# Two attentions in groups of a head pair and query tile, with joint maxima and split sums

## Chip, core and metric

One core of one Trainium2 chip runs the whole program. The metric is the device time of one execution in microseconds (us); the runs of a kernel are given by their median.

## What is computed

The program is two blocks in float32 on 512 tokens of width 1024. The change touches two attentions and what prepares the second one.

```
# first block, layer 2: 16 heads of 64, causal, with a decay
s = q_blk @ k.T * 64**-0.5 + cum_q - cum_k ; mask ; softmax ; @ v
# second block, layer 1: 16 query heads, 4 key/value heads, no mask
q = rope(rmsnorm(q)) ; k = rope(rmsnorm(k))
s = q @ k.T * 64**-0.5 ; softmax ; @ v ; @ w_o
```

The other layers (a state space mixer, four feed-forward parts, a gated MLP with mixing over tokens) stay as they are.

## The kernel before

Every large matrix product is made of three passes of split operands (high times high, high times low, low times high). SyncE loads weight units of 512 KB into a ring of four, ScalarE writes their high part (`whi`, line 544), GpSimd the low part (`wlo`, line 512), TensorE multiplies. Each engine has its program written out by hand, in its own order, and semaphores couple them; an engine never passes a wait.

**Attention** (`pe_attn`, `act_attn`, `dve_attn`, called twice: A = 0 causal with N = 128 to 512 columns by query tile, A = 1 with 512 always). A step n is one head and one query tile of 128 rows; n runs over 64 steps, the two heads of a pair taking turns. TensorE makes the scores of step n in one of three PSUM banks, VectorE takes the row maximum (`rowst`, line 1394), ScalarE the exponential with its row sum (line 797, into one of six `pbuf` buffers). Three steps later TensorE transposes the result block by block (line 1916), ScalarE copies the even steps to SBUF (line 805) and VectorE the odd ones (line 1401), and TensorE multiplies with v ("weighs", line 1889, 16 small matmuls per query tile of a pair) into one of two output banks. Once per pair VectorE writes the reciprocals of the eight sums, each repeated 64 times, in one operation of 512 columns (`rdup`, line 1409); TensorE transposes them (the "spread", line 1901), VectorE copies them (line 1383) and multiplies the pair's output with them (line 1386).

**Projection of the second attention** (`pe_t_x`, `act_qkv`, `dve_qkv`). TensorE makes three parts of four units: heads 0 to 7 (PSUM banks 0 to 3), heads 8 to 15 (banks 4 to 7), then keys and values (banks 0 to 3 again, once `q_step` has reached 16, which is VectorE's first read of the last token tile of part one). ScalarE squares a part when its four units are done; VectorE sums, inverts, and applies norm and rope in five operations for each of four token tiles, into `q_tok` and `k_tok`.

**Builds** turn rope results into `qS`, `kS` and `kL`, which hold q (high and low part, one above the other over the 128 partitions) and k high and k low. In the kernel before TensorE transposes q_tok or k_tok (line 1941), ScalarE writes the high part (lines 852, 854), VectorE subtracts it for the low part (lines 1496, 1499). Three builds come ahead of the attention, nine between its steps (`QK_AT`).

Of the kernel before, what the change touches and what calls it, by code (L numbers as in the profile page):

```python
# [46 lines left out]
SBANKS = 3  # L47
TBANK, OBANK, RBANK = 3, 5, 7
PSLOTS = 6
TSLOTS = 8  # L50
LEAD = 3
# [28 lines left out]
QK = [("q", 0, 4), ("q", 1, 5), ("k", 0, 6)]  # L80
QK_AT = {}
for _p in range(6):
    QK_AT[8 * _p + 1] = len(QK)
    QK.append(("q", _p + 2, 7))
    if _p % 2 == 0:
        QK_AT[8 * _p + 7] = len(QK)
        QK.append(("k", _p // 2 + 1, 7))
QK_OF = {(_kind, _x): _j for _j, (_kind, _x, _) in enumerate(QK)}
QK_DONE = [sum(2 if _kind == "q" else 1 for _kind, _, _ in QK[:_j + 1]) for _j in range(len(QK))]

# [29 lines left out]
def build_in(ctx, nc, a, out):  # L120
# [122 lines left out]
    v2 = arena("v2", [P, NT, 256], 64)  # L243
    q_tok = arena("q_tok", [P, NT, D], 48)
    oT2 = arena("oT2", [P, KD, T], 32)
    k_tok = arena("k_tok", [P, NT, 4, 2, HD], 68)
    cs = arena("cs", [P, NT, 2, HD], 76)
    qkg = arena("qkg", [P, 2, HD], 78)
    gcs = arena("gcs", [P, 2, NT, 2, HD], 79)
# [20 lines left out]
    def sem(name):  # L270
# [40 lines left out]
    at_rc = sem("at_recip_copied")  # L311

    q_sq, q_sum, q_std, q_step, v_ev, qk_tp, qk_hi, qk_lo, qkg_in, q_tab = (
        sem(n) for n in ("q_sq", "q_sum", "q_std", "q_step", "v_ev", "qk_tp", "qk_hi", "qk_lo", "qkg_in", "q_tab"))
# [472 lines left out]
    def act_attn(act, A, ptb, causal, hook=None, build=None):  # L787
        B, G = 64 * A, 32 * A
        for n in range(64 + LEAD):
            if n == 56 and hook:  # L790
                hook()
            if n < 64:
                N = (n % 8 // 2 + 1) * P if causal else T
                act.wait_ge(at_max, B + n + 1)
                if n >= PSLOTS:
                    act.wait_ge(at_tp, B + n - PSLOTS + 1)
                act.activation(pbuf[:, n % PSLOTS, 0:N], ps[:, n % SBANKS, 0:N], ACT.Exp, bias=rowst[:, 0, n:n + 1],
                               accum_out=rowst[:, 1, n:n + 1]).then_inc(at_exp, 1)
            m = n - LEAD
            if m >= 0 and m % 2 == 0:  # L800
                N = (m % 8 // 2 + 1) * P if causal else T
                act.wait_ge(at_tp, B + m + 1)
                if m >= TSLOTS:
                    act.wait_ge(at_pv, G + (m - TSLOTS) // 2 + 1)
                act.activation(ptb[:, m % TSLOTS, 0:N], ps[:, TBANK, 0:N], ACT.Copy).then_inc(at_pt_a, 1)
            if build:
                build(n - 1)
# [13 lines left out]
    def act_qkv(act):  # L821
# [4 lines left out]
        for e in range(13):  # L826
            if e < 12:
                act_whi(act, S + AHEAD, e, e % 4)
            if e and e % 4 == 0:
# [16 lines left out]
    def act_qk_hi(act, j):  # L846
        kind, x, bank = QK[j]
        act.wait_ge(qk_tp, j + 1)
        if kind == "q":
            for b in range(2):  # L850
                r = slice(64 * b, 64 * b + 64)
                act.activation(qS[r, (2 * x + b) % 8], ps[r, bank], ACT.Copy, scale=HD ** -0.5).then_inc(qk_hi, 1)
        else:
            act.activation(kS[:, x], ps[:, bank], ACT.Copy).then_inc(qk_hi, 1)
# [104 lines left out]
    def _(act):  # L959
# [41 lines left out]
        for t in range(NT):  # L1001
            act.wait_ge(res_done, 12 + t + 1)
            for h in range(2):
                if 2 * t + h:
# [9 lines left out]
                 build=lambda n: act_qk_hi(act, QK_AT[n]) if n in QK_AT else None)  # L1014
# [363 lines left out]
    def dve_attn(dve, A, oT, ptb, causal, hook=None, build=None):  # L1378
        B, G = 64 * A, 32 * A

        def pv_out(pr):
            dve.wait_ge(at_r, 8 * A + pr + 1)
            dve.tensor_copy(rinv_t[:], ps[:, RBANK]).then_inc(at_rc, 1)
            dve.wait_ge(at_pv, G + 4 * pr + 4)
            dve.wait_ge(at_rc, 8 * A + pr + 1)
            dve.tensor_tensor(oT[:, pr], ps[:, OBANK + pr % 2], rinv_t[:], ALU.mult).then_inc(at_o, 1)

        for n in range(64 + LEAD):
            if n == 58 and hook:
                hook()  # L1390
            if n < 64:
                N = (n % 8 // 2 + 1) * P if causal else T
                dve.wait_ge(at_s, B + n + 1)
                dve.tensor_reduce(rowst[:, 0, n:n + 1], ps[:, n % SBANKS, 0:N], AX.X, ALU.max, negate=True).then_inc(at_max, 1)  # L1394
            m = n - LEAD
            if m >= 0 and m % 2:
                N = (m % 8 // 2 + 1) * P if causal else T
                dve.wait_ge(at_tp, B + m + 1)
                if m >= TSLOTS:
                    dve.wait_ge(at_pv, G + (m - TSLOTS) // 2 + 1)  # L1400
                dve.tensor_copy(ptb[:, m % TSLOTS, 0:N], ps[:, TBANK + 1, 0:N]).then_inc(at_pt_d, 1)
            if build:
                build(n - 1)
            if n >= 9 and n % 8 == 1:
                pr = n // 8 - 1
# [5 lines left out]
            if n >= 14 and n % 8 == 6:  # L1411
                pv_out(n // 8 - 1)
        pv_out(7)
# [25 lines left out]
    def dve_qkv(dve):  # L1439
# [12 lines left out]
        for hh in range(3):  # L1452
# [10 lines left out]
            for t in range(NT):  # L1463
# [4 lines left out]
                twice = lambda x: x[:, 0:w].rearrange("p (h d) -> p h d", d=HD).unsqueeze(2).to_broadcast([P, nh, 2, HD])  # L1468
# [13 lines left out]
                if hh == 2:  # L1482
                    step(dve.tensor_tensor(k_tok[:, t], twice(ra), twice(rb), ALU.add))
                else:
                    step(dve.tensor_tensor(q_tok[:, t, hh * HALF:(hh + 1) * HALF], ra[:, 0:w], rb[:, 0:w], ALU.add))
        assert n == 60
        for j in range(3):
            dve_qk_lo(dve, j)

    def dve_qk_lo(dve, j):  # L1490
        kind, x, bank = QK[j]
        dve.wait_ge(qk_hi, QK_DONE[j])
        if kind == "q":
            for b in range(2):
                r, other = slice(64 * b, 64 * b + 64), slice(64 - 64 * b, 128 - 64 * b)
                dve.scalar_tensor_tensor(qS[other, (2 * x + b) % 8], ps[r, bank], HD ** -0.5, qS[r, (2 * x + b) % 8].bitcast(F32),
                                         ALU.mult, ALU.subtract).then_inc(qk_lo, 1)
        else:
            dve.tensor_tensor(kL[:, x], ps[:, bank], kS[:, x].bitcast(F32), ALU.subtract).then_inc(qk_lo, 1)
# [74 lines left out]
    def _(dve):  # L1574
# [56 lines left out]
        dve_attn(dve, 1, oT2, ptb2, False, hook=lambda: dve_first_splits(dve, "o", oT2),  # L1631
# [449 lines left out]
```

## Time and profile before

| | us |
|---|---|
| median of 3 runs | 3074.87 (3074.86 to 3079.23) |
| profiled execution | 3078.62 |
| its span, first to last instruction | 3076.5 |
| TensorE busy in the span | 2840.0 (92%) |
| VectorE, ScalarE, GpSimd busy | 1421.2, 1083.6, 1142.1 |
| mean granted TensorE clock | 0.966 |

The span is what the trace shows; the profiled execution's time has 2.1 us around it. A busy share tells little on its own here: the three engines behind TensorE matter where TensorE waits for them. Lines with L and a number are lines of the kernel above.

### The profile page before, as it was taken

To read this page: it belongs to the slowest core of one execution; us is meant where nothing else is said; L and a number is where in the kernel's file an instruction comes from. 1 tells how busy PE (TensorE), PEld (TensorE's weight loads), DVE (VectorE), ACT (ScalarE), POOL (GpSimd) and SP (SyncE) were. 2 spreads that over 40 slices of the span, in tenths; PEclk is the share of its full clock that TensorE was granted. 3 is DMA by queue.
4 is the path that set the end of the run, shared out by engine and by line. 5 is a ranking of instruction groups with operands and counts; after the bars stand their busy time and mean duration, and the time that the engine had idled before them with its cause. 6 is when DMAs were issued, how large, how long until landed. Compare 5 with 4: busy or idle time off the path is not lost.

```text
span 3076.5 us, 37311 instructions
## 1 busy us (share of the span) xinstructions
PE 2840.0 (92%) x13390; PEld 2312.3 (75%) x13390; DVE 1421.2 (46%) x1617; ACT 1083.6 (35%) x1529; POOL 1142.1 (37%) x466
## 2 busy tenths in 40 slices
PE   7998799999989988999967888999989988989999
PEld 6786577778867667778856667888878876878887
DVE  4323738775273657776357765123220145331232
ACT  4322233333333443334333544223344222432332
POOL 3442043344434113335423013445444434434443
PEclk9998799999989999999989999999999999999999
DMA  5331035763323004674212003323323331323232
GB/s 146 89 96 55 14 95 179 218 186 101 96 77 89 28 25 140 216 223 128 89 59 69 1 15 88 97 89 98 94 82 102 109 97 48 96 79 98 89 96 75
DMA packets 314313, 297.67 MB, mean 97 GB/s; under 512 B 11932, under 2 KB 246632, under 8 KB 314088
## 3 DMA queue, kind: packets, MB, share of 16 engines
q1 hardware_dynamic: 299784, 235.64, 26.0%
q10 hardware_dynamic: 14432, 60.70, 5.9%
q8 instruction: 65, 1.06, 0.1%
q14 instruction: 32, 0.26, 0.0%
HBM read 294.21 MB, written 2.10 MB: 96 GB/s over the span
## 4 chain that ended last, share of the span: by engine, by line
PE 46%; issue 35%; POOL 13%; DVE 5%; ACT 1%; POOLq 0%; DMA 0%; ACTq 0%; DVEq 0%
POOL wlo L512 13%; PE ps L1735 8%; PE ps L1736 8%; PE ps L1737 8%; PE ps L1652 6%; PE ps L1650 6%; PE ps L1651 6%; DVE nrm L1424 1%; DVE gk L1549 1%; PE ps L1889 0%; PE ps L1916 0%; PE ps L1761 0%; DVE rowst L1394 0%; PE ps L1763 0%; PE ps L1762 0%
## 5 line engine op out<-in xcount | busy, mean ns | idle before, releaser
L512 POOL TENSOR_TENSOR wlo<-raw,whi 128x1024 fp32r<-128x1024 f32 x444 | 1118.6, 2526 | 1875.9 <-ACT whi L544 1875.7
L1650 PE MATMUL ps<-xhi,whi 128*128 128x512 f32 x1824 | 714.0, 391 | 22.3 <-POOL wlo L512 20.8
L1651 PE MATMUL ps<-xlo,whi 128*128 128x512 f32 x1824 | 710.3, 389 | 0.0
L1652 PE MATMUL ps<-xhi,wlo 128*128 128x512 f32 x1824 | 709.9, 389 | 0.0
L544 ACT ACTIVATE whi<-raw 128x1024 fp32r<-128x1024 f32 x444 | 465.3, 1050 | 277.2 <-PE ps L1737 198.5
L1735 PE MATMUL ps<-whi,ahi 128*128 128x512 f32 x1184 | 465.5, 393 | 18.4 <-issue 11.2
L1736 PE MATMUL ps<-wlo,ahi 128*128 128x512 f32 x1184 | 463.6, 392 | 0.0
L1737 PE MATMUL ps<-whi,alo 128*128 128x512 f32 x1184 | 463.4, 391 | 0.0
L1650 PEld LDWEIGHTS ps<-xhi,whi 128*128 128x128 f32 x1824 | 342.6, 188 | 104.3 <-POOL wlo L512 32.1
L1652 PEld LDWEIGHTS ps<-xhi,wlo 128*128 128x128 f32 x1824 | 342.6, 188 | 71.5
L1651 PEld LDWEIGHTS ps<-xlo,whi 128*128 128x128 f32 x1824 | 342.6, 188 | 70.0
L1735 PEld LDWEIGHTS ps<-whi,ahi 128*128 128x128 f32 x1184 | 224.2, 189 | 67.9 <-issue 20.2
L1737 PEld LDWEIGHTS ps<-whi,alo 128*128 128x128 f32 x1184 | 224.0, 189 | 47.1
L1736 PEld LDWEIGHTS ps<-wlo,ahi 128*128 128x128 f32 x1184 | 224.2, 189 | 46.0
L1232 DVE TENSOR_TENSOR alo<-hid_mlp,ahi 128x1024 fp32r<-128x1024 f32 x60 | 78.7, 1312 | 233.3 <-ACT ahi L695 233.3
L1514 DVE SCALAR_TENSOR_TENSOR hid_mlp<-ps,relu 128x512 f32 (+1 forms) x64 | 44.3, 692 | 292.1 <-ACT relu L869 292.1
L1735 PE MATMUL ps<-whi,xhi 128*128 128x512 f32 x416 | 164.3, 395 | 7.6 <-DVE xlo L1045 4.6
L1736 PE MATMUL ps<-wlo,xhi 128*128 128x512 f32 x416 | 163.6, 393 | 0.0
L1737 PE MATMUL ps<-whi,xlo 128*128 128x512 f32 x416 | 163.5, 393 | 0.0
L695 ACT ACTIVATE ahi<-hid_mlp 128x1024 fp32r (+1 forms) x60 | 63.7, 1061 | 196.2 <-PE ps L1737 196.2
L768 ACT ACTIVATE gs<-gt 128x512 f32<-128x512 f32 x44 | 27.8, 632 | 291.8 <-DVE gt L1319 291.8
L869 ACT ACTIVATE relu<-ps 128x512 f32<-128x512 f32 x64 | 38.3, 599 | 240.1 <-PE ps L1652 240.1
(263 smaller groups left out, 3189.8 us busy)
## 6 DMA issues: line engine op xcount, KB each, us to landing
adaraw<-in_ada_w ACTq DMA_DIRECT2D x64, 768.0 KB, 5.8
raw<-in_ffn_w_up SPq DMA_DIRECT2D x88, 512.0 KB, 3.8
raw<-in_mlp_w_in SPq DMA_DIRECT2D x64, 512.0 KB, 4.0
raw<-in_mlp_w_out SPq DMA_DIRECT2D x64, 512.0 KB, 3.7
raw<-in_gmlp_w_in SPq DMA_DIRECT2D x48, 512.0 KB, 3.8
raw<-in_sc_ssm_w_in SPq DMA_DIRECT2D x44, 512.0 KB, 3.8
raw<-in_ffn_w_down SPq DMA_DIRECT2D x44, 512.0 KB, 3.7
raw<-in_fox_w_in SPq DMA_DIRECT2D x24, 512.0 KB, 3.7
```

What stands on the lines that cost most here:

```text
L512: pool.tensor_tensor(wlo[:, j], raw[:, j], whi[:, j].bitcast(F32), ALU.subtract).then_inc(w_lo, 1)
L544: act.activation(whi[:, s], raw[:, s], ACT.Copy).then_inc(w_hi, 1)
L695: act.activation(ahi[:, (m0 + j) % 2], x, ACT.Copy).then_inc(a_hi, 1)
L869: act.activation(relu[:, j % 2], ps[:, bank_f(j)], ACT.Relu).then_inc(relu_done, 1)
L1232: dve.tensor_tensor(alo[:, s], x, ahi[:, s].bitcast(F32), ALU.subtract).then_inc(a_lo, 1)
L1514: dve.scalar_tensor_tensor(hid_mlp[:, bass.ds(e, 1)], ps[:, bank_f(j):bank_f(j) + 1], 0.0, relu[:, j % 2:j % 2 + 1], ALU.max, ALU.mult).th ...
L1650: pe.matmul(out, lh, rh, start=start, stop=False)
L1651: pe.matmul(out, lh, rl, start=False, stop=False)
L1652: return pe.matmul(out, ll, rh, start=False, stop=stop)
L1735: pe.matmul(out, lh[:, k, c], wh[:, k], start=st, stop=False, skip_group_check=True)
L1736: pe.matmul(out, lh[:, k, c], wl[:, k], start=False, stop=False, skip_group_check=True)
L1737: ins = pe.matmul(out, ll[:, k, c], wh[:, k], start=False, stop=False, skip_group_check=True)
```

## The change

A group g is now one query tile of one head pair; there are 32. TensorE makes both scores (four score banks, two per group), VectorE takes the maxima of both heads in one operation over two banks, ScalarE makes both exponentials on that one signal. The transposes come two groups behind (LAG = 2), weighing one more group behind. There is one output bank instead of two. The sums are inverted as eight columns and then copied to 512.

The q and k parts are split before they are transposed: VectorE writes the roped tile to `roped` (two buffers), ScalarE copies its high part to `qsp` or `ksp`, VectorE subtracts the low part, and a build is then four transposes and one copy. `act_rope_hi(hh)` stands in ScalarE's block of the part after hh. Twelve builds come ahead of the attention (all four key heads, high and low, and q heads 0 to 3), twelve (one q head each) between its groups.

```diff
-SBANKS = 3
-TBANK, OBANK, RBANK = 3, 5, 7
+TBANK, OBANK, RBANK = 4, 6, 7
-LEAD = 3
+LAG = 2
-QK = [("q", 0, 4), ("q", 1, 5), ("k", 0, 6)]
+BUILDS = ([("q", _h, 4 + _h) for _h in range(4)]
+          + [(("kh", "kl")[_j % 2], _j // 2, 4 + _j % 4) for _j in range(8)])
+        BUILD_AT[4 * _p + 1 + 2 * _b] = len(BUILDS)
+        BUILDS.append(("q", 2 * _p + 4 + _b, RBANK))
...
 act_attn
+        for g in range(32 + LAG):
+            if g == 28 and hook:
+                hook()
+            if g < 32:
+                act.wait_ge(at_max, G + g + 1)
+                for n in (2 * g, 2 * g + 1):
+                    if n >= PSLOTS:
+                        act.wait_ge(at_tp, B + n - PSLOTS + 1)
+                    act.activation(pbuf[:, n % PSLOTS, 0:N], ps[:, n % 4, 0:N], ACT.Exp, bias=rowst[:, 0, n:n + 1],
+                                   accum_out=rowst[:, 1, n:n + 1]).then_inc(at_exp, 1)
+            w = g - LAG
+            if w >= 0:
+                act.wait_ge(at_tp, B + 2 * w + 1)
+                if w >= 4:
+                    act.wait_ge(at_pv, G + w - 3)
+                act.activation(ptb[:, 2 * w % TSLOTS, 0:N], ps[:, TBANK, 0:N], ACT.Copy).then_inc(at_pt_a, 1)
             if build:
-                build(n - 1)
+                build(g)
...
 act_qkv
+                if hh:
+                    act_rope_hi(act, hh - 1)
                 act.wait_ge(q_sum, 5 * hh + 4)
...
-        for j in range(3):
-            act_qk_hi(act, j)
+        for j in range(4):
+            act_build(act, j)
+        act_rope_hi(act, 2)
+        for j in range(4, FIRST_BUILDS):
+            act_build(act, j)
...
 dve_attn
+            if g < 32:
+                dve.wait_ge(at_s, G + g + 1)
+                dve.tensor_reduce(rowst[:, 0, 2 * g:2 * g + 2], ps[:, 2 * (g % 2):2 * (g % 2) + 2, 0:N], AX.X, ALU.max,
+                                  negate=True).then_inc(at_max, 1)
...
+            if g % 4 == 1 and g > 4:
+                pr = g // 4 - 1
                 dve.wait_ge(at_exp, B + 8 * pr + 8)
+                dve.reciprocal(rowst[:, 2, 8 * pr:8 * pr + 8], rowst[:, 1, 8 * pr:8 * pr + 8]).then_inc(at_rv, 1)
                 if pr:
                     dve.wait_ge(at_r, 8 * A + pr)
-                dve.reciprocal(rdup[:].rearrange("p i (b d) -> p (i b) d", d=HD),
-                               rowst[:, 1, 8 * pr:8 * pr + 8].unsqueeze(2).to_broadcast([P, 8, HD])).then_inc(at_rinv, 1)
+                dve.wait_ge(at_rv, 8 * A + pr + 1)
+                dve.tensor_copy(rdup[:].rearrange("p i (b d) -> p (i b) d", d=HD),
+                                rowst[:, 2, 8 * pr:8 * pr + 8].unsqueeze(2).to_broadcast([P, 8, HD])).then_inc(at_rinv, 1)
+            if g % 4 == 2 and g > 4:
+                pv_out(g // 4 - 1)
...
 dve_qkv
+                step(dve.tensor_tensor(x, ra[:, 0:w], rb[:, 0:w], ALU.add))
+                if t:
+                    dve_rope_lo(dve, hh, t - 1)
+            dve_rope_lo(dve, hh, NT - 1)
...
+    def dve_rope_lo(dve, hh, t):
+        dve.wait_ge(q_hi, 4 * hh + t + 1)
...
 pe_attn
+        for g in range(32 + LAG + 1):
+            if g < 32:
+                if g >= 2:
+                    pe.wait_ge(at_exp, B + 2 * g - 2)
+                for b in range(2):
+                    ins = scores(pe, 2 * (g // 4) + b, g % 4, 2 * (g % 2) + b)
+                ins.then_inc(at_s, 1)
+            w = g - LAG
+            if 0 <= w < 32:
+                pe.wait_ge(at_exp, B + 2 * w + 2)
+                for b in range(2):
+                    if w:
+                        pe.wait_ge(at_pt_d if b else at_pt_a, G + w)
+                    for c in range(w % 4 + 1 if causal else NT):
+                        ins = pe.transpose(ps[:, TBANK + b, c * P:(c + 1) * P],
+                                           pbuf[:, (2 * w + b) % PSLOTS, c * P:(c + 1) * P], ident)
+                    ins.then_inc(at_tp, 1)
+            if w >= 1:
+                weigh(w - 1)
+                if w % 4 == 0:
+                    spread(w // 4 - 1)
             if build:
-                build(n)
+                build(g)
```

## Rows read from the trace of the kernel before

**Rows 1.** The page, chain that ended last: shares of the span by engine.
```profile
PE 46%; issue 35%; POOL 13%; DVE 5%; ACT 1%; POOLq 0%; DMA 0%; ACTq 0%; DVEq 0%
```
**Rows 2.** Busy time by stretch: PE, PEld, DVE, ACT, POOL, then granted clock, DMA, GB/s.
```profile
1678.00:1686.00 8.00, 5.51 (x17) 4.17 (x18) 5.38 (x8) 3.44 (x6) 0.00 (x0) 0.51 0.00 0
1681.50:1822.00 140.50, 114.04 (x963) 88.39 (x964) 107.52 (x135) 74.01 (x178) 2.35 (x1) 0.95 0.00 1
```
**Rows 3.** Timeline, first attention: start, duration, engine, line, operation [idle before].
```profile
1093.63 3.34 DVE L1409 RECIPROCAL rdup<-rowst 128x512 f32<-128x512 f32 x1
...
1105.75 3.34 DVE L1409 RECIPROCAL rdup<-rowst 128x512 f32<-128x512 f32 x1
...
1112.78 1.02 PE L1927 MATMUL ps<-kh,qh 128*128 128x512 f32 x2
...
1113.70 0.39 PE L1916 MATMUL ps<-consts,pbuf 128*128 128x128 f32 x2
```
**Rows 4.** Who waited for whom, 1022 to 1122: total us, times, longest.
```profile
PEld ps L1916 <- ACT pbuf L797: 10.1, 15, 1.6
```
**Rows 5.** Groups by line and shape, VectorE, whole span: busy us, mean ns | idle before.
```profile
L1409 DVE RECIPROCAL rdup<-rowst 128x512 f32<-128x512 f32 x16 | 53.5, 3345 | 0.7 <-ACT pbuf L797 0.6
...
L1165 DVE TENSOR_TENSOR mbuf<-ps,sm 128x1024 f32<-128x1024 f32 x8 | 9.8, 1220 | 1.6 <-PE ps L1835 1.6
...
L1272 DVE RECIPROCAL rstd<-std 128x4 f32<-128x4 f32 x4 | 0.7, 178 | 2.3 <-ACT std L742 2.3
```
**Rows 6.** Timeline, second attention: a stretch without a reciprocal, and its end.
```profile
1709.57 0.59 ACT L805 ACTIVATE ptb<-ps 128x512 f32<-128x512 f32 x1
...
1710.05 0.69 ACT L797 ACTIVATE pbuf<-ps,rowst 128x512 f32<-128x512 f32 x1
1710.30 0.63 PE L1916 MATMUL ps<-consts,pbuf 128*128 128x128 f32 x4 [0.93 <-ACT ptb L805]
...
1711.00 0.39 PE L1935 MATMUL ps<-kL,qS 128*128 128x512 f32 x1
...
1711.37 0.61 ACT L805 ACTIVATE ptb<-ps 128x512 f32<-128x512 f32 x1
1711.43 0.69 DVE L1394 TENSOR_REDUCE rowst<-ps 128x1 f32<-128x512 f32 x1 [0.78 <-PE ps L1935]
1711.76 1.09 PE L1889 MATMUL ps<-ptb,v 128*64 128x128 f32 x16
...
1712.15 0.69 ACT L797 ACTIVATE pbuf<-ps,rowst 128x512 f32<-128x512 f32 x1 [0.17 <-DVE rowst L1394]
...
1712.78 0.50 PE L1934 MATMUL ps<-kS,qS 128*128 128x512 f32 x1
...
1713.12 0.40 PE L1935 MATMUL ps<-kL,qS 128*128 128x512 f32 x1
...
1814.35 1.03 PE L1916 MATMUL ps<-consts,pbuf 128*128 128x128 f32 x8
...
1815.32 1.09 PE L1889 MATMUL ps<-ptb,v 128*64 128x128 f32 x16
```
**Rows 7.** Timeline, projection and rope of the second attention.
```profile
1633.48 0.68 DVE L1475 TENSOR_TENSOR qn<-ps,hsum 128x512 f32<-128x512 f32 x1
...
1635.59 0.69 DVE L1485 TENSOR_TENSOR q_tok<-ra,rb 128x512 f32<-128x512 f32 x1
1636.20 0.68 DVE L1475 TENSOR_TENSOR qn<-ps,hsum 128x512 f32<-128x512 f32 x1
...
1645.28 0.39 PE L1735 MATMUL ps<-whi,xhi 128*128 128x512 f32 x1
...
1646.51 2.04 ACT L836 ACTIVATE sqb<-ps 128x512 f32<-128x512 f32 x4
...
1667.25 1.21 ACT L836 ACTIVATE sqb<-ps 128x256 f32<-128x256 f32 x4 [4.33 <-PE ps L1737]
...
1669.37 0.37 ACT L841 ACTIVATE hsum<-hsum,eps_ln 128x16 f32<-128x16 f32 x1
```

More of the change, by code:

```diff
@@ L788, in act_attn @@
         B, G = 64 * A, 32 * A
-        for n in range(64 + LEAD):
-            if n == 56 and hook:
+        for g in range(32 + LAG):
+            if g == 28 and hook:
                 hook()
[L792 to L805, printed above, removed]
+            if g < 32:
+                N = (g % 4 + 1) * P if causal else T
+                act.wait_ge(at_max, G + g + 1)
[6 more added lines that the diff above has]
+            if w >= 0:
+                N = (w % 4 + 1) * P if causal else T
+                act.wait_ge(at_tp, B + 2 * w + 1)
+                if w >= 4:
+                    act.wait_ge(at_pv, G + w - 3)
+                act.activation(ptb[:, 2 * w % TSLOTS, 0:N], ps[:, TBANK, 0:N], ACT.Copy).then_inc(at_pt_a, 1)
             if build:
-                build(n - 1)
+                build(g)
     def act_square(act, s, h, tiles_ready):
@@ L1376, in dve_fv, with dve_attn @@
                 dve.tensor_copy(vtok[:, t, h * HALF:(h + 1) * HALF], ps[:, 4 * h + t]).then_inc(fv_ev, 1)
-    def dve_attn(dve, A, oT, ptb, causal, hook=None, build=None):
+    def dve_attn(dve, A, oT, ptb, causal, hook=None):
         B, G = 64 * A, 32 * A
@@ L1385, in pv_out @@
             dve.wait_ge(at_rc, 8 * A + pr + 1)
-            dve.tensor_tensor(oT[:, pr], ps[:, OBANK + pr % 2], rinv_t[:], ALU.mult).then_inc(at_o, 1)
-        for n in range(64 + LEAD):
-            if n == 58 and hook:
+            dve.tensor_tensor(oT[:, pr], ps[:, OBANK], rinv_t[:], ALU.mult).then_inc(at_o, 1)
+        for g in range(32 + LAG):
+            if g == 29 and hook:
                 hook()
[L1391 to L1405, printed above, removed]
+            if g < 32:
+                N = (g % 4 + 1) * P if causal else T
+                dve.wait_ge(at_s, G + g + 1)
+                dve.tensor_reduce(rowst[:, 0, 2 * g:2 * g + 2], ps[:, 2 * (g % 2):2 * (g % 2) + 2, 0:N], AX.X, ALU.max,
+                                  negate=True).then_inc(at_max, 1)
+            w = g - LAG
+            if w >= 0:
+                N = (w % 4 + 1) * P if causal else T
+                dve.wait_ge(at_tp, B + 2 * w + 2)
+                if w >= 4:
+                    dve.wait_ge(at_pv, G + w - 3)
+                dve.tensor_copy(ptb[:, (2 * w + 1) % TSLOTS, 0:N], ps[:, TBANK + 1, 0:N]).then_inc(at_pt_d, 1)
+            if g % 4 == 1 and g > 4:
+                pr = g // 4 - 1
@@ L1481, in dve_qkv @@
                 dve.wait_ge(q_step, n)
[L1482 to L1485, printed above, removed]
+                step(dve.tensor_tensor(x, ra[:, 0:w], rb[:, 0:w], ALU.add))
+                if t:
+                    dve_rope_lo(dve, hh, t - 1)
+            dve_rope_lo(dve, hh, NT - 1)
         assert n == 60
[L1487 to L1497, printed above, removed]
-        else:
-            dve.tensor_tensor(kL[:, x], ps[:, bank], kS[:, x].bitcast(F32), ALU.subtract).then_inc(qk_lo, 1)
+        for j in range(4, FIRST_BUILDS):
+            kind, x, bank = BUILDS[j]
+            if kind == "kl":
+                dve.wait_ge(bd_tp, j + 1)
+                dve.tensor_copy(kL[:, x], ps[:, bank]).then_inc(bd_ev_d, 1)
+    def dve_rope_lo(dve, hh, t):
+        dve.wait_ge(q_hi, 4 * hh + t + 1)
+        x = roped[:, t % 2]
+        if hh < 2:
+            dve.tensor_tensor(qsp[:, t, 8 * hh:8 * hh + 8, 1], x.rearrange("p (h d) -> p h d", d=HD),
+                              qsp[:, t, 8 * hh:8 * hh + 8, 0].bitcast(F32), ALU.subtract).then_inc(q_lo, 1)
+        else:
+            dve.tensor_tensor(ksp[:, t, :, 1], x[:, 0:4 * HD].rearrange("p (h d) -> p h d", d=HD).unsqueeze(2)
+                              .to_broadcast([P, 4, 2, HD]), ksp[:, t, :, 0].bitcast(F32), ALU.subtract).then_inc(q_lo, 1)
     def dve_gate(dve, s):
@@ L1883, in weigh @@
             pe.wait_ge(at_pt_d, G + g + 1)
-            if i == 0 and pr >= 2:
-                pe.wait_ge(at_o, 8 * A + pr - 1)
+            if i == 0 and pr:
+                pe.wait_ge(at_o, 8 * A + pr)
             last = i if causal else NT - 1
@@ L1954, in pe_mod, with pe_build_at @@
+    def pe_build_at(pe, g):
+        if g in BUILD_AT:
+            j, pr = BUILD_AT[g], g // 4
+            pe.wait_ge(bd_ev_a, BUILT_ACT[j - 1])
+            if g % 4 == 1 and pr >= 2:
+                pe.wait_ge(at_o, 8 + pr - 1)
+            if g % 4 == 3 and pr >= 1:
+                pe.wait_ge(at_o, 8 + pr)
+            pe_build(pe, j)
     def pe_mod(pe, L):
```

145 lines of the change are left out of this document (67 added, 78 removed).

## The prediction

> **What bounds the kernel now.** I read the page first, for the chain that ended last, then the busy time by stretch, then the timelines of the three stretches that the change touches. The chain is TensorE's own work or its issue time for 81% of the span [rows 1]: whatever makes TensorE wait costs time, and the other engines cost nothing until they do. The change touches three stretches, all on one path because TensorE works through them in order: the first (causal) attention, 1022.5 to 1127.6; the projection with its rope, up to the first score of the second attention at 1681.5; and the second attention, 1681.5 to 1822.0, where TensorE is busy 114 of 140.5 us [rows 2]. The first attention repeats every 12.12 us per head pair [rows 3], and in 1022:1122 (8.2 such periods) its weight loads wait 10.1 us for exponentials [rows 4]; one of its 15 waits, 1.6 us, is in the tail, so about 1.1 us per pair is waiting and 11.0 us is TensorE's own work. The second attention takes 140.5 us for eight pairs, some 16.5 us each between reciprocals.
>
> **Prices.** The reciprocal of 512 columns takes 3.34 us, 16 times. It becomes one of 8 columns (0.18 us for 4 columns) and a copy of 512 columns, at most 0.7 us. VectorE saves about 2.5 us per pair [rows 5]. The Trainium skill ("VectorE: DVE Perf Modes", Rules for kernel authors) says to minimize the count of operations and not to split; by that rule alone one instruction more would cost some tenths. The row says that here the width of the divide is what costs. The joint maximum reads two PSUM banks, which no maximum does now; the bounds are 1.22 us, the two-bank operation of 1024 columns, and 1.38, twice the 0.69 of one maximum [rows 5, 6]. I take 1.22, since it has one fixed part and not two: the maximum saves little, but the exponentials of both heads now start only when it is done.
>
> **Second attention, period.** I write s for the start of a group's scores on TensorE. The first score's two matmuls take 0.34 and 0.23, the second's 0.22 each (full pace, 512 columns at 2.4 GHz); its last matmul ends 0.39 after it starts and VectorE starts 0.04 later [rows 6]. So the maximum starts at s + 1.22, the exponentials at s + 2.47 (1.22 + 0.03 handoff). Two exponentials take 1.34. Only behind them stands the copy of the transposed pair two groups earlier: 0.59, and 0.14 more until the next group's transposes may start [rows 6]. That is s + 4.54. Eight transposes with their gap take 0.97 (1814.35 to 1815.32), weighing 1.02 (1711.76 to 1712.78), then come the scores of the group after next: s + 6.53, so 3.27 us per group, against 3.01 of TensorE's own work (1.02 + 0.97 + 1.02). Even groups carry two builds per pair (0.35 each, four transposes): 13.8 per pair. Odd ones carry the spread (0.39) and a late maximum: VectorE copies and multiplies the old pair's output for 1.40 behind the spread, until s + 5.15, while the next maximum is due at s + 4.67. That gives 13.1 + 0.4 + 0.5 = 14.0 per pair, now 16.5. Walking it from the first score: warm start to group 13 at 42.1, four more pairs to group 29 at 98.0, then both splits of the hook (2.0 us on ScalarE, 2.3 on VectorE, partly covered), tail and last spread: 115.6 us instead of 140.5. **Gain 24.9.** What goes away is the wait behind the reciprocal, and the VectorE subtraction of the q and k builds between scores.
>
> **First attention.** The same round, with sizes by query tile. The long case is the group of tile 3: one score is 0.92 (1112.78 to 1113.70), the maximum starts at s + 2.04, then 1.25, two exponentials 1.34, copy of a 256-column tile 0.37 + 0.14: s + 5.14. TensorE would be there at s + 3.5 (scores 1.84, four transposes 0.54, four weighings 0.37, the next group's scores 0.75), estimates scaled from the same rows [rows 3, 6]. It waits 1.6 us once per pair; the other three groups come in time. Period 11.0 + 1.6 = 12.7, now 12.12: +0.6, over eight pairs +4.9. In the tail the last copy no longer stands behind a 3.34 us reciprocal, and the pipeline is one group longer: -2.5. **Loss 2.4.** One bank for the output instead of two costs nothing here: the first weighing of a pair comes at s + 2.4, the multiply ends at s + 1.8; in the second attention the margin is only 0.1 us.
>
> **Projection and rope.** Here work is added: twelve subtractions of 512 columns on VectorE (0.69 each, 0.61 back to back, as 1635.59 to 1636.20) [rows 7], twelve copies on ScalarE, 12 leading builds instead of 3. Their order matters more. In the half for heads 0 to 7, VectorE's first low part follows tile 1, but ScalarE issues the high part only in its block for the next half, behind TensorE's unit 8 and four squares. So VectorE stops at 1636.2, where tile 2 starts now, and goes on at 1649.15 (squares from 1646.51 for 2.04, copy 0.63) [rows 7]. Tile 3 is read from PSUM at 1649.15 + 0.61 + 2.72 + 0.61 = 1653.1 (2.72 is 1633.48 to 1636.20), done 1653.8. TensorE's third part waits for exactly this and starts at 1653.85 instead of 1645.28: 8.6 us idle. Its work is 21.9 us, ending now at 1667.2 [rows 7]. Idle time also costs clock: TensorE stands still from 1668 to 1678, and the granted clock is then 0.51 until 1686, the 1.2 GHz level [rows 2]. I take 5.3 us at half rate, 2.6 us lost. End: 1678.4. The Trainium skill ("TensorE: Matmul & The Clock Gate", HAM oscillation) says that such waits re-throttle TensorE; without it the sum would be 2.6 lower.
>
> The same happens once more. VectorE has finished tiles 0 and 1 of the second half by 1670 and stops until squares, v copies (2.12, 1667.25 to 1669.37) and the high part are issued: 1678.45 + 2.12 + 0.63 = 1681.2. Two tiles and four low parts: 1689.25. The key part's reduce, root and reciprocal take 2.1 (estimated from today's 2.4, without the wait for the v copies): 1691.4; four tiles at some 1.7 and the low parts: 1700.7. Only then come the eight key builds. Each is 0.7 at the low clock (0.4 at the high one, half of the 0.97 of eight transposes), and the last needs 1.1 for its transposes to land and 0.69 for VectorE's copy: first score at 1707.3 (1705.0 at the high clock) instead of 1681.5. **Loss 25.8.** The builds' evictions on ScalarE (0.5 to 0.6 per two builds) stay behind TensorE. SyncE's loads are unmoved: the four units of the third part are ready, and the next weights are wanted only after the attention.
>
> **Sum.** -24.9 + 25.8 + 2.4 = +3.3 on a span of 3076.5, 3079.8. The profiled execution took 3078.62, of which 2.1 lies around the span; the median of the three runs shown is 3074.87. Added to that median: 3078.2. About 0.2%, 6.15 us, is what a measurement of this kernel can tell from no change (the three runs differ by 4.4).
>
> **Rivals.**
> A, faster: the attentions run at TensorE's own pace, because the copy is not what the transposes wait for. Then the first attention takes 11.0 per pair and loses its tail (-11 instead of +2.4) and the second 13.1 (another -7): 3058. For it: VectorE's load falls by 2.5 per pair. Against: the round of 4.54 + 1.99 is summed from durations in the trace, and it is longer than twice 3.01.
> B, slower: the round through both exponentials is longer than summed, because the two-bank maximum or a handoff costs more. It is gone through 16 times in the second and 8 times in the first attention where it binds; 0.12 us more per round already passes +6.15, and 0.3 us more gives 3085.4. For it: I have no row of a two-bank maximum, the margin at the output bank is 0.1, and sums of this kind leave out small waits.
> C, faster: VectorE's stop in the rope doesn't reach TensorE (the third part's banks are free earlier than I read) and only the added low parts (12 x 0.61 = 7.3), and builds (8 more, 5) count, 12.3 instead of 25.8: 3064.7. Against it: the wait for step 16 stays in the kernel, and both engines work strictly in order.
> D: the reciprocal of 8 columns costs as much as that of 512. Then the second attention gains almost nothing: over 3090. The 4-column row speaks against it [rows 5].
>
> **Chances.** Forecast 0.52 (its own range 3072 to 3084: the clock term 2.6 in the projection, 2.3 in the builds, 0.1 us per round), of which 0.44 lies within 0.2% and 0.08 above. B 0.28, D 0.02, A 0.11, C 0.07. That makes slower 0.38, same 0.44, faster 0.18. The range reaches from C's value to a B of 0.4 us per round, 3064 to 3088; below it lies A, above it D and the worst of B, together under 0.2.
>
> **What would show it.** In the changed profile: TensorE idle some 8 us in the projection, ended by a VectorE multiply of the rope, and a second half low clock after it; VectorE idle from about 1636 to 1649, ended by ScalarE; the first score of the second attention 24 to 28 us later counted from the start of the projection; then 14.0 us per pair, with TensorE's transposes waiting for ScalarE's copy. In the first attention 12.7 per pair and one wait of 1.6 us for that copy. I am wrong if the pairs take 13.1 and 11.0 (A), if no idle stretch stands in the projection (C), or if the reciprocals are still long (D).

## The result and the profile after

The changed kernel takes 3088.63 us (median of 11 runs, 3084.89 to 3092.23), the kernel before 3079.09 us (median of 11, 3074.86 to 3083.41). The ratio is 1.003, 95% interval 1.0022 to 1.0037: slower by 9.5 us or 0.3%. The profiled execution took 3091.49 us with a span of 3089.7, 13.2 us more than the span before. I cut both spans at the same five events: first score of the first attention, first matmul of the output projection behind it, first score of the second attention, first matmul of the projection behind that, end.

| us | before | after | difference | forecast |
|---|---|---|---|---|
| ahead of the first attention | 1022.5 | 1025.6 | +3.1 | 0 |
| first attention | 105.1 | 114.3 | +9.2 | +2.4 |
| up to the second attention | 553.9 | 578.1 | +24.2 | +25.8 |
| second attention | 140.5 | 116.7 | -23.8 | -24.9 |
| behind it | 1254.5 | 1255.0 | +0.5 | 0 |

The ratio's interval leaves out 1, so the change is slower by a little. The first and last lines have the same code in both kernels. In twelve other executions (below) the first is 1017.6 to 1025.8 and the last 1254.5 to 1257.1, so neither says anything of the change.

**Projection and rope.** Timeline of VectorE and TensorE, where [rows 7] show the same events without a stop:

```profile
1646.13 0.69 DVE L1502 TENSOR_TENSOR roped<-ra,rb 128x512 f32<-128x512 f32 x1
1659.63 0.69 DVE L1517 TENSOR_TENSOR qsp<-roped,qsp 128x512 fp32r<-128x512 f32 x1 [12.81 <-ACT qsp L860]
...
1691.23 0.69 DVE L1517 TENSOR_TENSOR qsp<-roped,qsp 128x512 fp32r<-128x512 f32 x1 [13.31 <-ACT qsp L860]
...
1664.30 0.79 PE L1756 MATMUL ps<-whi,xhi 128*128 128x512 f32 x1 [8.32 <-DVE qn L1495]
...
1695.90 3.56 PE L1975 MATMUL ps<-consts,qsp 128*128 128x128 f32 x16 [7.57 <-DVE qn L1495]
1710.68 6.43 PE L1975 MATMUL ps<-consts,ksp 128*128 128x128 f32 x32 [11.22 <-DVE ksp L1520]
1717.99 0.47 PE L1957 MATMUL ps<-kS,qS 128*128 128x512 f32 x1 [0.88 <-DVE kL L1511]
```

VectorE has two roped tiles by 1646.8 and stands for 12.81 us for ScalarE's high copy (L860), and for 13.31 us once more in the second half. TensorE ends the second part at 1655.8 and stands 8.32 us for VectorE's first read of the fourth tile. Then it starts at half pace: a matmul begins every 0.43 us instead of every 0.23, until 1668.3. It stands again before the first four builds (7.57) and the eight key builds (11.22). The granted clock by stretch (columns as in [rows 2]):

```profile
1656.00:1664.00 8.00, 0.00 (x0) 0.00 (x0) 4.30 (x8) 4.67 (x8) 2.34 (x1) 0.64 0.35 121
1664.00:1672.00 8.00, 7.70 (x25) 6.20 (x26) 7.38 (x14) 0.95 (x2) 0.00 (x0) 0.72 0.01 2
1672.00:1688.00 16.00, 16.00 (x73) 13.18 (x71) 5.82 (x9) 3.18 (x3) 7.52 (x3) 1.00 0.22 69
```

**Second attention.** One group's round, from its first score at 1760.40 to the next transposes:

```profile
1760.40 0.50 PE L1957 MATMUL ps<-kS,qS 128*128 128x512 f32 x1
...
1761.64 1.23 DVE L1413 TENSOR_REDUCE rowst<-ps 128x2 f32<-128x1024 f32 x1 [1.47 <-PE ps L1958]
...
1762.90 0.69 ACT L800 ACTIVATE pbuf<-ps,rowst 128x512 f32<-128x512 f32 x1 [1.62 <-DVE rowst L1413]
...
1764.24 0.60 ACT L808 ACTIVATE ptb<-ps 128x512 f32<-128x512 f32 x1
...
1764.98 1.07 PE L1937 MATMUL ps<-consts,pbuf 128*128 128x128 f32 x8
```

The transposes come at s + 4.58 (forecast 4.54), s being the start of the group's first score as in the prediction. The joint maximum takes 1.23 (forecast 1.22). A pair takes 14.04 us from one reciprocal to the next (forecast 14.0). The reciprocal and its copy, in the same groups of VectorE's work as [rows 5]:

```profile
L1429 DVE COPY rdup<-rowst 128x512 f32<-128x512 f32 x8 | 3.4, 428 | 0.8
L1425 DVE RECIPROCAL rowst<-rowst 128x8 f32<-128x8 f32 x8 | 1.5, 192 | 0.0
```

What TensorE waited for here (total us, times, longest), the three largest before and the largest after:

```profile
PE ps L1916 <- ACT ptb L805: 9.3, 8, 3.7
PE ps L1916 <- DVE ptb L1401: 9.2, 7, 3.1
PE ps L1901 <- DVE qS L1496: 5.5, 5, 1.1
...
PE ps L1937 <- ACT ptb L808: 7.8, 12, 1.9
```

The clock changed too. Before, the granted clock was 0.95 in this stretch, with TensorE busy 114.0 us [rows 2]; after, it is full, with nearly the same number of instructions:

```profile
1718.00:1835.00 117.00, 107.78 (x977) 85.10 (x978) 74.79 (x96) 71.28 (x176) 1.36 (x1) 1.00 0.01 1
```

**First attention.** The widest group, and the wait behind it:

```profile
1109.78 1.02 PE L1949 MATMUL ps<-kh,qh 128*128 128x512 f32 x2
...
1111.88 1.23 DVE L1413 TENSOR_REDUCE rowst<-ps 128x2 f32<-128x1024 f32 x1 [0.40 <-PE ps L1950]
...
1114.48 0.38 ACT L808 ACTIVATE ptb<-ps 128x256 f32<-128x256 f32 x1
...
1115.00 1.01 PE L1937 MATMUL ps<-consts,pbuf 128*128 128x128 f32 x6 [1.54 <-ACT ptb L808]
```

That is s + 5.22 (forecast 5.14) and a wait of 1.54 (forecast 1.6). The widest maximum comes every 12.89 us where nothing disturbs it, and twice only after 14.5. The extra 1.6 us is pace: the transposes behind the wait above take 1.01 us for six, 0.85 in the other pairs. TensorE alone by stretch (time, busy, count, granted clock):

```profile
1064.00:1077.00 13.00, 11.46 (x91) 1.00 0.01 2
1077.00:1090.00 13.00, 11.46 (x86) 0.93 0.01 1
1090.00:1103.00 13.00, 11.46 (x82) 0.94 0.00 1
...
1116.00:1129.00 13.00, 11.12 (x77) 0.89 0.00 0
1129.00:1140.00 11.00, 6.48 (x55) 0.82 0.01 1
```

Who waited for whom in all of the first attention, TensorE's matmuls, before and after ([rows 4] show the weight loads, a different queue, so they don't compare with this):

```profile
PE ps L1916 <- ACT ptb L805: 5.3, 7, 1.4
...
PE ps L1937 <- ACT ptb L808: 13.0, 9, 2.4
```

### The profile page after: what moved, and what is told of

Read it like the earlier page. It is cut to its first block, busy times and chain, and to the rows that moved or that the text cites. A ratio compares the mean times of both kernels' runs of the same rounds, so it can differ in the third digit from the quotient of the medians.

```text
span 3089.7 us, 37251 instructions
## 1 busy us (share of the span) xinstructions
PE 2849.7 (92%) x13438; PEld 2323.1 (75%) x13438; DVE 1364.7 (44%) x1565; ACT 1087.8 (35%) x1541; POOL 1141.5 (37%) x466
## 4 chain that ended last, share of the span: by engine, by line
PE 46%; issue 34%; POOL 12%; DVE 5%; ACT 1%; POOLq 0%; DMA 0%; ACTq 0%; DVEq 0%
POOL wlo L514 12%; PE ps L1756 8%; PE ps L1758 8%; PE ps L1757 8%; PE ps L1673 6%; PE ps L1672 6%; PE ps L1671 6%; PE ps L1910 1%; PE ps L1937 1%; DVE nrm L1444 1%; DVE gk L1571 1%; DVE rowst L1413 0%; PE ps L1782 0%; PE ps L1784 0%; PE ps L1783 0%
## 5 line engine op out<-in xcount | busy, mean ns | idle before, releaser
L1671 PE MATMUL ps<-xhi,whi 128*128 128x512 f32 x1824 | 714.6, 392 | 22.2 <-POOL wlo L514 20.7
```

The source lines that it names most:

```text
L1671: pe.matmul(out, lh, rh, start=start, stop=False)
```

## The experiments

The medians are of 5, 11, 5, 5, 11, 4, 8, 4, 4, 11, 11 and 4 runs, in the order of the experiments. Each ratio is to the kernel before as it ran in the same session (medians 3078.95, 3080.73 and 3079.99 for experiments 1 to 4, 5 to 8 and 9 to 12); differences in us are between medians as printed, so 1 or 2 us between sessions are in them. Stretches are from one profiled execution of each kernel, in the order of the table above: first attention, up to the second, second attention.

**1. Copy ahead of the exponentials.**

```diff
 act_attn, for each g
+            [wait for the transposes; copy ptb of group g - 2]
             [wait for the maxima; two exponentials of group g]
-            [wait for the transposes; copy ptb of group g - 2]
```

> The changed kernel with one edit: ScalarE copies the transposed pair of two groups back before, not behind, the two exponentials of a group. Theory (the round through the joint maximum, both exponentials and only then the copy holds TensorE's transposes; 13.0 us of such waits in the first attention, 7.8 in the second, and the 3.2 us of low clock behind them): most of it goes, 18 us (14 to 22) off the changed kernel, about 3070; the first attention repeats every 11.4 us instead of 12.9, the second every 13.1 to 13.3 instead of 14.0, and no low clock is left inside the first. Rival (TensorE is held by something else of the round, the exponentials that free the score banks or VectorE's late maximum, and the copy only happens to end last): the waits change their name, and the time stays within 3 us, 3086 to 3092.

Measured: 3063.44 us (3061.03 to 3064.31), ratio to before 0.9947 (0.9933 to 0.996): 25.2 us off the changed kernel. Stretches 96.4, 578.8, 106.0. The widest maximum comes every 11.19 us, 0.5 us of waits for the copy are left in the first attention, and behind the start TensorE is busy without a gap and at full clock, as here:

```profile
1064.00:1077.00 13.00, 13.00 (x98) 1.00 0.00 0
```

The rival fell: the waits went, they did not change their name. The size is above my bound (14 to 22): not most, but nearly all of the waits and of the low clock inside the pairs went (13.0 + 3.2 + 7.8 = 24.0).

**2. Four roped tiles.** `roped` gets four buffers, and VectorE's low parts stand behind the fourth tile.

```diff
-                if t:
-                    dve_rope_lo(dve, hh, t - 1)
-            dve_rope_lo(dve, hh, NT - 1)
+            for t in range(NT):
+                dve_rope_lo(dve, hh, t)
```

> The changed kernel with four buffers for the roped tiles instead of two, and VectorE's four low parts behind the fourth tile instead of one behind each tile, so that VectorE finishes a half of the rope without waiting for ScalarE; ScalarE's order is as it was. Theory (VectorE's stop for ScalarE's high copy is what TensorE's third part waits for, 8.3 us and 1.9 us of low clock behind it; the second stop delays the key part by two tiles, 5.4 us): 15.5 us off the changed kernel (12 to 19), about 3073, TensorE's third part starts without a wait for the rope. Rival (only the added work counts and the stop is hidden by TensorE's own work): less than 3 us. Between them (the third part starts in time but the key part waits for ScalarE's late high copies anyway): 10 us.

Measured: 3075.42 us (3071.19 to 3078.17), ratio 0.9988 (0.9979 to 0.9997): 13.2 off the changed kernel, inside the theory's range. Stretches 112.3, 564.3, 116.7. Of the difference 2.0 us lie in the first attention, whose code is the same. TensorE's third part starts without a wait; where the changed kernel has waits of 8.3, 7.6 and 11.2 us before the attention, two are left:

```profile
PE ps L1974 <- DVE ksp L1519: 13.7, 1, 13.7
PE ps L1974 <- DVE qn L1495: 3.0, 1, 3.0
```

**3. The reciprocal over 512 columns in the changed kernel.**

```diff
-                dve.reciprocal(rowst[:, 2, ...8], rowst[:, 1, ...8]).then_inc(at_rv, 1)
-                dve.tensor_copy(rdup, rowst[:, 2, ...8] to 512)
+                dve.reciprocal(rdup, rowst[:, 1, ...8] to 512)
```

> The changed kernel with the reciprocal of before in it: one over 512 columns, 3.3 us, instead of 8 columns and a copy. Theory (VectorE's maximum of the next group comes 2 us late behind it and is on the round): 16 us more in the second attention and 4 to 12 in the first, 20 to 28 us more, about 3112. Rival (the grouping by pairs, one round for two heads, made the gain, and VectorE's idle time hides a long reciprocal): less than 5 us more, 3089 to 3094.

Measured: 3103.79 us (3099.18 to 3104.99), ratio 1.0078 (1.0064 to 1.0092): 15.2 more than the changed kernel. Stretches 116.4, 579.3, 126.1. Between the two theories: the groups hide some of a 3.34 us reciprocal, not all of it. The second attention loses 9.4 us, not 16, and the first 2.1, not 4 to 12; in the first attention the pairs grow from 12.89 to 13.30 us.

**4. The split alone**, in the kernel before (the third experiment's diff the other way round).

> The kernel before with one edit: the reciprocal over 512 columns is split into one over 8 columns and a copy; its order, its three score banks, its rope and its builds are untouched. Theory (the long reciprocal is what the second attention's waits stand behind): 2.3 us per pair, 18 us off the kernel before in the second attention and 2 to 4 in the first, where part of TensorE's waits of 1.1 us per pair goes, 20 us in all (12 to 24), about 3059. Rival (three score banks and steps of one head hold the second attention, whatever the reciprocal takes): less than 6 us off, 3073 to 3079.

Measured: 3055.63 us (3048.59 to 3057.16), ratio 0.9916 (0.9902 to 0.9929): 23 us under the kernel before. Stretches 100.9, 554.6, 119.8. The second attention loses 20.7 us of its 140.5 by this one edit, where the whole change takes 23.8. There TensorE's waits for VectorE's copy (L1401) fall from 9.2 to 0.6 us and those for its low parts of q (L1496) go; those for ScalarE's copy stay (9.3 and 8.2). The granted clock of the stretch rises from 0.95 to 0.97, so a part of the 20.7 is clock. The Trainium skill (VectorE: DVE Perf Modes, Rules for kernel authors) advises to keep the count of operations low. Here two of 0.19 and 0.43 us beat one of 3.34 us.

**5. High copies ahead of the squares**, on top of the second.

```diff
+                if hh:
+                    act_rope_hi(act, hh - 1)
                 act.wait_ge(unit_done, S + 4 * hh + 4)
...
-                if hh:
-                    act_rope_hi(act, hh - 1)
```

> The second experiment's kernel (four roped tiles) with ScalarE's high copies of a half ahead of the next part's squares instead of behind them. Theory (with four tiles VectorE still stood 3.7 us before the low parts, until ScalarE had done four squares): the key part, which ends last before the attention, comes 3.6 us earlier; 3 to 5 us off the second experiment, about 3072. Rival (the squares now wait for the fourth roped tile and give the time back, VectorE being the bound of the stretch from there on): within 1.5 us of the second experiment.

Measured: 3074.16 us (3071.53 to 3078.06), ratio 0.9982 (0.9973 to 0.9991): 1.3 us under the second, whose stretch up to the attention was 564.3 and is now 563.3. The intervals overlap; the size is the rival's, and no gain is shown. The first attention, whose code is the changed one, took 109.7 us here, and its waits are the same; this time none of its stretches behind the start is below full clock:

```profile
1075.00:1088.00 13.00, 11.46 (x92) 1.00 0.01 1
1088.00:1101.00 13.00, 11.46 (x92) 1.00 0.01 2
1101.00:1114.00 13.00, 11.46 (x91) 1.00 0.00 0
1114.00:1128.00 14.00, 11.57 (x107) 1.00 0.00 1
```

**6. One, two and five together.**

> The changed kernel with the edits of the first, second and fifth experiment together. The stretches are separate, so if the causes are, the savings add up: 25.2 + 13.2 + 3.6 us off the changed kernel's 3088.6, about 3047 (3043 to 3051). Rival (one cause behind both, the low clock, or the attention's start overlapping the rope's end): under 36 us in all, over 3052.

Measured: 3046.45 us (3046.02 to 3046.51), ratio 0.9889 (0.9874 to 0.9904): 42.2 off the changed kernel, the sum of the measured parts being 39.7 (25.2 + 13.2 + 1.3). Stretches 96.4, 563.0, 106.0. The savings add up, so the rival of one cause behind both fell.

**7. Two maxima instead of the joint one**, the copy last as changed.

```diff
-                dve.wait_ge(at_s, G + g + 1)
-                dve.tensor_reduce(rowst[:, 0, 2 * g:2 * g + 2], [both banks], AX.X, ALU.max, negate=True)
+                for n in (2 * g, 2 * g + 1):
+                    dve.wait_ge(at_s, B + n + 1)
+                    dve.tensor_reduce(rowst[:, 0, n:n + 1], ps[:, n % 4, 0:N], AX.X, ALU.max, negate=True)
```

(ScalarE waits for each in turn, TensorE signals each score.)

> The changed kernel, ScalarE's order as changed (copy behind both exponentials), but with a maximum, a signal and a wait for each head of a group instead of the joint ones. Theory (the joint maximum lengthens the round of 5.1 us at the widest group of the first attention by 1.2 us, and that of the second attention by 0.9): TensorE's wait in the first attention falls from 1.54 to about 0.4 per pair, 9 us and most of the 3.2 us of low clock less, and the second attention loses its waits, 6 us: about 3071 (3067 to 3076). Rival (the second exponential sets the round, and its maximum ends only 0.5 us earlier than the joint one): 4 us in the first and 3 in the second, 3078 to 3084. Third (the joint maximum saves as much as it delays): 3086 to 3091.

Measured: 3072.83 us (3067.71 to 3073.85), ratio 0.9972 (0.9961 to 0.9982): 15.8 off the changed kernel, as the theory had it. Stretches 101.3, 580.7, 109.0. Two maxima take 1.29 us together where the joint one takes 1.23, so it saves 0.06 us and holds the first exponential back by some 0.5. In the first attention the waits for the copy fall from 13.0 to:

```profile
PE ps L1937 <- ACT ptb L808: 4.7, 8, 1.3
```

**8. Split and copy first in the order of before.**

```diff
 act_attn of before, for each n
+            [copy of step n - 3]
             [exponential of step n]
-            [copy of step n - 3]
```

> The kernel before, in its own order by single heads, with the split reciprocal of the fourth experiment and with ScalarE's copy ahead of the exponential of a step. Theory (in the order of before, too, TensorE's waits are for a copy queued behind an exponential: 5.3 us in the first attention and 8.2 in the second with the split alone): 12 us (9 to 15) off the fourth experiment's 3055.6, about 3044. Rival (three score banks hold it: an exponential 0.4 us later frees its bank later): within 3 us of the fourth experiment.

Measured: 3042.43 us (3041.07 to 3043.27), ratio 0.9877 (0.9862 to 0.9892). That is 13.2 off the fourth experiment, so the theory held. Stretches 94.9, 553.9, 112.1. Two small edits to the kernel before, without groups or a new rope, save 37 us. The copy's move was not run without the split.

**9. The groups on the rope of before, copy first.** Attention functions of the first experiment; in the kernel before's builds, key heads 1 to 3 are built behind groups 4p + 1 (p even) and q pairs behind 4p + 3.

```diff
+    if _p % 2 == 0:
+        QK_AT[4 * _p + 1] = len(QK)
+        QK.append(("k", _p // 2 + 1, 7))
+    QK_AT[4 * _p + 3] = len(QK)
+    QK.append(("q", _p + 2, 7))
```

> The changed attentions (groups, joint maxima, split reciprocal) with ScalarE's copy ahead of the exponentials as in the first experiment, on the projection, rope and builds of before (three leading builds, low parts subtracted from PSUM on VectorE during the attention). Theory (each stretch's price is its own): first attention 96.4 us, between the attentions 554, second attention 107 (106.0 as in the first experiment, about 1 us for VectorE's subtractions between maxima), the rest as ever: 3037 (3033 to 3042). Rival (the low parts during the attention come late and hold the spread and the builds, which is why they would be worth moving out): second attention 112 or more, 3042 and over.

Measured: 3037.48 us (3036.84 to 3038.62), ratio 0.9863 (0.9848 to 0.9878). Stretches 96.5, 552.5, 107.2: each of them within 1.5 us of its theory. The rival fell.

**10. The same with the copy last**: the attention's half of the change alone.

> As the ninth experiment, but with the copy behind both exponentials, as changed: the attention's half of the change alone, without its half in the rope. Theory (the rope's half is what loses 24 us, the attention's half gains 15): 3065 (3060 to 3070), 14 us under before. Rival (the halves need each other; the subtractions on VectorE lengthen the round with the copy last): 3072 and over.

Measured: 3072.7 us (3068.46 to 3074.03), ratio 0.9976 (0.9967 to 0.9985). Stretches 116.2, 552.4, 123.1. The time is the rival's; its reason is so only in part. The second attention takes 6.4 us more than in the changed kernel (123.1 against 116.7). Of these, 4.0 stand at its start: from the first score to the first reciprocal it is 21.2 us against 17.2, at a granted clock of 0.83 against 1.00 (TensorE alone):

```profile
1686.00:1708.00 22.00, 17.58 (x113) 0.83 0.00 1
```

That leaves 2.4 us for VectorE's subtractions between the maxima, and some low clock near the end is in these too. With the copy first (the ninth) the rope of before costs 1.2 us here (107.2 against 106.0): 2.7 more at the start and 1.5 less in the pairs. So the change's rope costs 24 to 26 us between the attentions and gives back 6 at most, the larger part of it at the start of the attention, which the kernels with the rope of before reach at low clock.

**11. A busy wait.** Twelve transposes of the identity into the spread bank where TensorE waits in the first attention.

```diff
+            if causal and g % 4 == 0 and 8 <= g < 32:
+                pe.wait_ge(at_rc, g // 4 - 1)
+                for c in range(12):
+                    pe.transpose(ps[:, RBANK, c % 4 * P:(c % 4 + 1) * P], ident, ident)
```

> The changed kernel with twelve transposes of the identity into the idle spread bank where TensorE waits 1.5 us per pair in the first attention; the computation is otherwise the same. Theory (the stretches at low clock come of the idle waits, in some executions and not in others: three executions with the same first attention took 114.3, 112.3 and 109.7 us): the first attention takes 109 to 110 us with no slice under full clock after its start up to the last group, and the median falls by 1 to 4 us to about 3086. Rival (the low clock comes of something else): nothing changes, within 1 us of 3088.6, and low slices are left inside; or the transposes take longer than the wait and it gets slower.

Measured: 3085.48 us (3082.14 to 3089.86), ratio 1.0018 (1.0009 to 1.0028): 3.1 under the changed kernel, with work added; the two intervals (1.0009 to 1.0028 and 1.0022 to 1.0037) just overlap. The first attention took 111.3 us, more than the theory's 110. There is full clock in all of its filled periods and low clock in the tail, which has no fill:

```profile
1102.00:1115.00 13.00, 12.80 (x103) 1.00 0.00 1
1115.00:1128.00 13.00, 7.62 (x64) 0.83 0.00 0
1128.00:1134.00 6.00, 5.06 (x13) 0.52 0.10 12
```

This fits the theory and doesn't show it: experiments 2 and 5 have full clock inside their pairs too, with the waits left as they were.

**12. Two maxima, copy first**, on the ninth.

> The ninth experiment's kernel with a maximum for each head as in the seventh. Theory (with the copy first, TensorE's own work is the bound, and a shorter round gives nothing more): within 1.5 us of the ninth. Rival (the joint maximum costs time of its own, whatever the copy's place): 4 us or more off the ninth.

Measured: 3035.56 us (3034.89 to 3037.03), ratio 0.9858 (0.9843 to 0.9873): 1.9 under the ninth. Stretches 95.7, 553.1, 106.1. Near the theory, a little more than its 1.5, and with overlapping intervals: with the copy first, a cost of the joint maximum is not shown. It is the fastest version here, 1.4% under the kernel before.

## Why the prediction was wrong, and where it was right

It said 3078.2 us (3064 to 3088), most likely no measurable change. The result is 3088.6, slower. The mechanisms were right nearly everywhere; the balance was not. It was lost in two places: the terms of the first attention, where the tail was mis-sized and the low clock put at nothing, and the base to which the sum was added.

**Second attention: right.** Forecast -24.9, measured -23.8. The round came at 4.58 for 4.54. The two things that I said would go away did: the wait behind the reciprocal (the split gives 20.7 us by itself, experiment 4) and the subtractions between scores. The rest of the change, without the split, gives 14.4 (140.5 to 126.1, experiment 3). They overlap; together they give 23.8. A third thing went away that I didn't name: my durations were those of full clock, and the stretch before had 0.95. TensorE's busy time fell by 6.2 us with it. The joint maximum costs 7.8 us in this stretch with the copy last (experiment 7), and 1.1 with the copy first (107.2 and 106.1, experiments 9 and 12).

**Projection and rope: right.** Forecast +25.8. From the end of TensorE's second part to the first score it is 62.2 us (1655.8 to 1718.0), before 36.2 (1645.3 to 1681.5): +26.0. VectorE's first stop (12.8 us, summed as 12.9) and TensorE's idle time (8.3, summed as 8.6) came as summed. The low clock behind it ended after some 4 us, where I had 5.3. VectorE's second stop was longer, 13.3 for 11.2, because it began earlier; counted from the end of TensorE's second part it ended within 0.5 us of the sum. Four buffers take back 13.9 of the 24.2 us of the whole stretch between the attentions (experiment 2). What stays, 9 to 10 us, was not taken apart by a run; the added low parts and leading builds stand there.

**First attention: the terms that failed.** Forecast +2.4 as 12.7 against 12.12 us per pair (+4.9) and a tail of -2.5. The cause is the round that I gave: joint maximum, two wide exponentials, and only then the copy. Moving the copy out of it takes 17.9 us from this stretch (experiment 1); two maxima, with the copy still last, take 13.0 (experiment 7). The first of the two terms was of the right size. The tail's was not, and a third term was left out:
- The pairs: up to the second score of the last widest tile it is 91.9 us before (1022.5 to 1114.39) and 96.4 in the undisturbed execution of experiment 5 (1022.8 to 1119.19), +4.5 for +4.9. A period is 12.89, not 12.7. TensorE's own work is 11.19 (experiment 1) and not 11.0, which with the wait of 1.54 makes 12.73; 0.16 us are not accounted for. I had taken the 1.1 us of waiting per pair from the weight loads; the matmuls' waits for the copy before are 5.3 us in all. The first pair starts up 0.9 us faster and takes the difference back.
- The tail: from there to the next projection it is 13.2 us before (to 1127.62) and 13.3 after (to 1132.47), 0 instead of -2.5. The long reciprocal is gone from it, but the joint maximum and both exponentials stand before the copy that the last transposes want, a wait of 2.4 us.
- The low clock: I counted it in the rope and left it out here, though I had forecast the very waits that bring it. The same code took 109.7, 112.3 and 114.3 us in three executions: behind the start without low clock, with it in the tail alone, and with two stretches more inside. So without it the difference is +4.6 (109.7 to 105.1), and the profiled execution has 4.6 more. What it costs the median is not shown; filling the waits gave 3.1 us back (experiment 11).

**The base.** I added my sum to the median of three runs, 3074.87; the median of eleven is 3079.09. That moved the forecast by 4.2 us of the 10.4 by which it missed, though not its sign: the measured difference is +9.5, the sum said +3.3. Of the 6.2 us between them, the low clock may be about 3.1 (taken from experiment 11), the first attention's tail 2.5 and the second attention 1.1; the pairs of the first gave 0.4 and the stretch between the attentions 1.6 less than forecast. That makes 4.7; the rest, 1.5, was not placed and is within the scatter of the runs.

**The rivals.** B, that the round costs more than summed, has the right sign and not quite the right place: the round itself was longer by 0.08 in the first attention and 0.04 in the second, under the 0.12 from which I let it decide. A fell as well, since the transposes do wait for the copy; with the copy moved TensorE does run at its own pace (106.0 and 96.4 us). C and D fell: the stop reached TensorE, and the narrow reciprocal is 0.19 us.

## What to carry to other kernels

- On an engine that works in order, put the work that another engine already waits for ahead of the work whose input isn't there yet. ScalarE's copy could run while it stood for the maxima; behind the exponentials it held TensorE. That was 25 us here, and the same move gave 13 us in the kernel before, on top of the split reciprocal.
- A producer that needs another engine's step in the middle wants as many buffers as that engine is late: with two tiles VectorE stood for 12.8 and 13.3 us, with four for 3.7 us and then not at all.
- A change with a gain and a loss is worth splitting before it is judged. One line of this change, the split reciprocal, beats the whole change by 33 us when it is put alone into the kernel before.

## What the runs showed of the hardware

**Short waits can go with low clock, but not in every execution.** Five kernels here have the joint maximum and the copy last and wait some 1.5 us once per pair of the first attention: the changed one and experiments 2, 3, 5 and 10. In one profiled execution of each, TensorE fell to the 1.2 GHz level inside the pairs twice in the changed kernel (the slices of 0.93 to 0.89 above) and three times in experiment 10 (0.87 in a slice of 13 us each), and never in the other three. It never did in the nine kernels with shorter waits, filled ones or none. The scatter of the times settles nothing: eleven runs of the changed kernel cover 7.3 us, but eleven of experiment 11, with filled waits, 7.7, and five of experiment 4 cover 8.6. Those of experiments 6, 8, 9 and 12 cover 0.5 to 2.2, with only four runs each. The Trainium skill (TensorE: Matmul & The Clock Gate, A second HAM failure mode: psum-queue depth-cycling) tells of such oscillation from short idle times; two of the five traces agree. What was new to me is that it differs between executions of the same code, so one profile doesn't show its price.

**A VectorE operation on two SBUF tiles waits for GpSimd.** VectorE's multiplication of 512 columns takes 0.69 us. If both inputs lie in SBUF and it begins during GpSimd's subtraction, it ends 0.5 to 0.6 us after that, here 2.17 us long; the one just before it, which reads PSUM and begins during the same subtraction, takes 0.68 as ever. From the second experiment:

```profile
1646.16 2.73 POOL L514 TENSOR_TENSOR wlo<-raw,whi 128x1024 fp32r<-128x1024 f32 x1 [2.79 <-ACT whi L546]
...
1646.55 0.68 DVE L1495 TENSOR_TENSOR qn<-ps,hsum 128x512 f32<-128x512 f32 x1
1647.27 2.17 DVE L1497 TENSOR_TENSOR ra<-qn,gcs 128x512 f32<-128x512 f32 x1
```

The Trainium skill (SBUF — State Buffer, Who interferes with whom) says that VectorE's second pair of ports is shared with GpSimd and held by one at a time; the trace agrees. It has a price here: in the rope, six VectorE operations of the second experiment are lengthened so, by 12.3 us together, and two in the changed kernel, by 3.6, where VectorE stood still instead. A part of what four buffers could give back may go there; no run separates it.
